# Two input tiles, then the first conditioning group, then the other tiles: a new order at the head of a one-layer decoder step

## What is computed

```python
mod = jnp.einsum('bd,de->be', jax.nn.silu(c), w_ada) + b_ada
sh1, sc1, g1, sh2, sc2, g2 = [m[:, None, :] for m in jnp.split(mod, 6, axis=-1)]
h = x * (1 + sc1) + sh1
z = jnp.einsum('btd,de->bte', h, w_in) + b_in
a_glu, q, k, v, qi, ki, wi, uv, gate_logits = jnp.split(z, SPLIT_OFFSETS, axis=-1)
```

## Time and profile before

| | |
|---|---|
| median of 3 runs | 1046.58 us (1044.06 to 1046.66) |
| the profiled execution's own time | 1057.31 us |
| its span, first to last instruction | 1055.4 us |
| TensorE busy | 998.1 us (95%) |
| VectorE busy | 548.5 us (52%) |
| ScalarE busy | 198.9 us (19%) |
| GpSimd busy | 254.2 us (24%) |
| mean granted clock of TensorE | 0.970 |
| moved by DMA | 214.98 MB, mean 204 GB/s |

### The profile page before, as it was taken

One profiled execution on the slowest core, in us unless ns is written; L12 is line 12 of the kernel. 1 busy time (PEld: TensorE's weight loads), 2 busy tenths in 40 slices (PEclk: granted clock), 3 DMA queues, 4 the chain that ended last, 5 costly groups with the idle time before them and its releaser, 6 DMA issues. The chain is left out here.

```text
span 1055.4 us, 23402 instructions
## 1 busy us (share of the span) xinstructions
PE 998.1 (95%) x9475; PEld 719.8 (68%) x9475; DVE 548.5 (52%) x1381; ACT 198.9 (19%) x474; POOL 254.2 (24%) x284
## 2 busy tenths in 40 slices
PE   5999999999999999899999999977999999999995
PEld 4677777557776767576777764554776777677763
DVE  1131899984457888976456815687233121011137
ACT  1110012213222323232111110111111111111104
POOL 0010002824121223123335620000211212422123
PEclk8998999999999999899999999976999999999998
DMA  9964742653605215014072336242799999899995
GB/s 307 308 139 114 240 161 82 217 206 122 238 21 164 77 31 195 20 46 126 11 191 69 120 98 271 70 189 101 306 423 416 357 410 396 347 383 396 389 277 113
DMA packets 94003, 214.98 MB, mean 204 GB/s; under 512 B 23572, under 2 KB 48407, under 8 KB 89797
## 3 DMA queue, kind: packets, MB, share of 16 engines
q1 hardware_dynamic: 78388, 186.20, 49.5%
q0 software_dynamic: 6672, 19.67, 6.2%
q10 hardware_dynamic: 8841, 7.64, 2.6%
HBM read 201.12 MB, written 16.92 MB: 207 GB/s over the span
## 5 line engine op out<-in xcount | busy, mean ns | idle before, releaser
L2120 PE MATMUL banks<-arena 128*128 128x288 f32 (+6 forms) x1774 | 427.6, 396 | 6.3 <-issue 2.5
L2120 PEld LDWEIGHTS banks<-arena 128*128 128x128 f32 (+1 forms) x1774 | 317.1, 191 | 108.9 <-issue 32.4
L2520 PE MATMUL banks<-arena 128*32 128x256 f32 x3136 | 186.7, 384 | 4.1 <-issue 2.9
L2520 PEld LDWEIGHTS banks<-arena 128*32 128x32 f32 x3136 | 131.7, 110 | 48.5 <-issue 8.1
L2048 DVE TENSOR_TENSOR arena<-arena,banks 128x128 f32<-128x128 f32 x49 | 14.1, 288 | 222.7 <-ACT arena L1353 222.5
L2542 PE MATMUL banks<-arena 128*32 128x256 f32 x1568 | 100.2, 379 | 1.5 <-issue 0.8
L1051 POOL DMA_INDIRECT expert_rows<-arena,ints x44 | 43.0, 977 | 196.9 <-ACT arena L1364 192.8
L993 POOL TENSOR_SCALAR arena<-arena 128x288 f32<-128x288 f32 x46 | 44.9, 975 | 168.2 <-ACT arena L1275 102.1
L1430 DVE SCALAR_TENSOR_TENSOR arena<-arena 128x512 f32<-128x512 f32 x120 | 82.0, 743 | 0.0
L2542 PEld LDWEIGHTS banks<-arena 128*32 128x32 f32 x1568 | 61.5, 109 | 21.7 <-issue 6.4
L2134 PE MATMUL banks<-arena 128*128 128x288 f32 x256 | 69.9, 431 | 2.7 <-DVEq L1448 2.7
(11 more groups left out here) (321 smaller groups left out, 998.4 us busy)
## 6 DMA issues: line engine op xcount, KB each, us to landing
arena<-in_w_e_gate SPq DMA_DIRECT2D x16, 2048.0 KB
arena<-in_w_e_up SPq DMA_DIRECT2D x16, 2048.0 KB
arena<-in_w_e_down SPq DMA_DIRECT2D x16, 2048.0 KB
arena<-in_w_ada SPq DMA_DIRECT2D x8, 2048.0 KB, 10.3
arena<-in_w_in SPq DMA_DIRECT2D x8, 2048.0 KB, 9.7
arena<-in_w_ada SPq DMA_DIRECT2D x8, 1024.0 KB, 11.6
arena<-in_x_prompt SPq DMA_DIRECT2D x8, 512.0 KB, 7.0
arena<-in_w_in SPq DMA_DIRECT2D x14, 256.0 KB, 8.2
```

Source lines behind the costliest of these rows:

```text
L2120: last = pe.matmul(out, a, b, start=k == 0, stop=k == len(pairs_) - 1)
L2520: last = pe.matmul(out, HG[:, g % 2, k, a:a + BLK], both_weights(i, k, c), start=k == 0, stop=k == KT - 1)
```

## The change

In the list of steps, conditioning group 0 moves ahead of tiles 2 and 3, the samples and the parameters, and ahead of all halves 1, which move behind `acc 0`. In SP's order, the two loads of group 0 move ahead of those of tiles 2 and 3, the samples and the page ids. Nothing is computed anew and no bytes are added.

```diff
-    plan = [("cT",)] + [("xT", t, z) for t in range(4) for z in range(2)] + [("xTs",), ("par",), ("adp", 0), ("mT", 0), ("mod", 0)]
+    plan = [("cT",), ("xT", 0, 0), ("xT", 1, 0), ("adp", 0), ("xT", 2, 0), ("xT", 3, 0), ("xTs",), ("par",), ("mT", 0), ("mod", 0)]
     for g in range(3):
-        plan += [("acc", 2 * g, 0, 6), ("adp", g + 1), ("acc", 2 * g + 1, 0, 3), ("mT", g + 1), ("mod", g + 1), ("acc", 2 * g + 1, 3, 6)]
+        plan += [("acc", 2 * g, 0, 6)] + ([("xT", t, 1) for t in range(4)] if g == 0 else []) + [("adp", g + 1), ("acc", 2 * g + 1, 0, 3), ("mT", g + 1), ("mod", g + 1), ("acc", 2 * g + 1, 3, 6)]
     plan += [("acc", 6, 0, 6)]
@@
         for t in range(NT):
+            if t == 2:
+                first_conditioning(0)
             src = I["x_prompt"][0, t * P:t * P + P, :] if t < 4 else I["x_sample"].rearrange("b t f -> (b t) f")
             sp.dma_start(X[0:rows_of(t), t, :], src).then_inc(ev(f"tile_in{t}"), 16)
@@
         for g in range(4):
-            first_conditioning(g)
+            if g > 0:
+                first_conditioning(g)
             a_columns(2 * g, 2, slice(0, P), f"a_in{g}")
             a_columns(2 * g, 2, slice(512, 512 + 2 * P), f"a_in{g}")
```

## The result

The changed kernel takes 1052.39 us (median of 20 runs), the kernel before 1049.21 us (20 runs beside them). The ratio is 1.0036 with a 95% interval of 1.0023 to 1.0049, that is +3.8 us (+2.4 to +5.1); the plain difference of the two medians is +3.2. The forecast was +3.8 us, which made 1050.4 on the three runs then known. The direction and the size of the difference held. Several terms of the sum did not, and that their errors nearly cancelled is luck.

The account below looks back on a forecast made before the run. TensorE was taken to bound the kernel, its head passing through nearly one to one: +0.3 us at `acc 0` and +3.8 for second-half flips made +4.1, reduced to +3.8 over the 1046.58 us median: 1050.4 us, range 1046.5 to 1053.

Parts of the forecast that it names:

- The bound: After 32 us TensorE bounds the kernel, so what its head gains or loses goes through nearly one to one.
- The landing of `adp 0`: First conditioning group's load, issued behind tile 1, lands at 17.5 us instead of 21.3, kept late by the conv weights' packets.
- Half clock at `adp 0`: After TensorE's wait the first conditioning group again runs at half clock, taking 3.64 us, to 21.1 us.
- Flips, samples and hand-over to VectorE's `mT`: Behind `adp 0`: 2.8 us of flips, samples and parameters at full clock, 1.55 us to VectorE's `mT`, +0.6 for the clock.
- From there to `acc 0`: From VectorE's `mT` to the start of the first projections: 1.71 us, as in the kernel before.
- `acc 0`: First projections start at 27.8 us, 0.3 later than before, and keep their length of 4.87 us, mostly at half clock.
- The second halves: Four groups of flips between `acc 0` and `adp 1`, 1.90 us for two: 3.8 us, all on the path.
- The second halves in under 3 us: Sign of a wrong prediction: the four groups of flips behind `acc 0` take less than 3 us.
- The sum at `adp 1`: Second conditioning group starts 4.1 us later, at about 36.4 instead of 32.35 us: +0.3 at `acc 0`, +3.8 for flips.
- The early landing: Rival, chance 0.11: `adp 0` lands early enough to win, at 13.8 us by bytes; 1043.5 to 1046.3 us.
- The clock's rival: Rival, chance 0.19: clock does not fall at `acc 0`, which takes 3.19 us; +1.8 us in all, 1048.3 us.
- the cold case: Rival, chance 0.13: flips behind `adp 0` wholly at half clock, second halves partly; +5.8 to +7.5 us, 1052.4 to 1054.1.

Follow-up runs that it names:

- e4: Changed kernel with the conv weights' load cut into 16 and 15 rows; 1.0014 of the time of the kernel before (+1.5 us).
- e5: Kernel before with the conv weights' load cut into 16 and 15 rows; 0.9982 of the time of the kernel before (-1.9 us).
- e7: Kernel before with idle matmuls in TensorE's waits ahead of the parameters, `adp 0` and `acc 0`; 0.9973 of the time before (-2.8 us).
- e10: Changed kernel with six idle matmuls ahead of `adp 0` and two ahead of `acc 0`; 1.0007 of the time before (+0.7 us).
- e3: Changed kernel with the second halves of tiles 0 and 1 flipped ahead of `adp 0`; 1.0012 of the time before (+1.3 us).
- e6: Changed loads, conv load cut; tiles 0 and 1's second halves and parameters ahead of `adp 0`, `mT` right behind it; 0.9968 of the time before (-3.4 us).

## Why the prediction was right, step by step

- *The bound* held: a shift of the head goes through, as the table's two columns of differences show for all ten kernels, each within its interval. The intervals are 2.7 to 5 us wide, so this holds no closer than that.
- *The landing of `adp 0`* was taken at 17.5 and was 18.8 us: 1.3 us mis-sized. The reason given for its lateness, the conv weights' packets, was the right one (e4), but their price was taken from the old order, where the cut is worth 1 to 2 us; in the new one it is 3.2 to 4.2.
- *Half clock at `adp 0`*: 3.64 us, as forecast. *Flips, samples and hand-over to VectorE's `mT`*: 22.62 to 26.78 = 4.2 us, forecast 2.8+1.55 and 0.6 for the clock, 0.8 us too much: the flips ran at full speed, and the 2.8 us were a pace of half clock already (see below). *From there to `acc 0`*: 1.71 us, as forecast. `acc 0` started at 28.49, forecast 27.8: +1.5 from the release of `adp 0` (18.98 us for 17.5), -0.8 from the flips and the hand-over.
- *`acc 0`* was left at 4.87 us and took 5.68. The step weighed only a change of the clock for the better. The half clock at this step lasts differently long from kernel to kernel (4.58 to 6.11 us for the twelve records where it does not stay away); what sets that is open.
- *The second halves* failed in size: 3.8 forecast, 2.8 measured. "The second halves in under 3 us" stood among the prediction's own signs of being wrong, and it came: they are exposed, as the forecast says, but cheaper. The 1.90 us for two were read from the stretch at 9 to 15 us, which I took to be at full clock because the column said so. But eight flips at 6.34 us took 1.97 us, and here, at 34.01 us, 1.03: the head of the kernel before was at half clock too, and what I took for the pace of full clock was not.
- The sum at `adp 1` was +4.1 and is +4.48: +0.7 from the start of `acc 0`, +0.7 from its length (from its start to the next step's 5.52 us, before 4.80), -1.0 from the second halves. The near agreement is luck.
- *The rivals.* The early landing (at 13.8 us) did not come, but e4 shows that it was to be had: with the conv weights' load cut it is 14.6 us, and the change is then level in the head with the kernel before as it was (not with that kernel and the same cut, e5). The clock's rival did not come in the profiled execution; it came in two of the eight kernels without idle matmuls, and was put at 0.19. e7 and e10 show what full clock at both steps is worth at `adp 1`: some 3.4 us in the old order (2.6 and the 0.7 of the later release) and 4.3 in the new (4.1-0.8+1.0, for the earlier release and for what the idle matmuls took). What the cold case named, flips at half clock, did not come (and it took the second halves at 3.4 us, where the forecast has 3.8); what grew was the half clock at `acc 0` itself, which no case had priced.
- The Trainium skill's rule on work cut up by waits (TensorE: Matmul & The Clock Gate, section "HAM oscillation — how this bites in real kernels") pointed to the cold case; e7 shows the rule at work, with 1.7 us at `adp 0` and 1.7 at `acc 0`, though the wait ahead of `acc 0` is one for VectorE and not for a load. Since both orders have both waits it speaks only a little against the change.

## What to carry to other kernels

A step that stands in a wait is free, and moving a critical load forward empties that wait of its cheap work: first count what is left to fill the new, longer wait, and put there whatever already has its inputs (e3, e6). When a load lands late for its bytes, look for a small transfer of another queue in the same time and try it cut: 31 rows as 16 and 15 brought `adp 0` 3.2 to 4.2 us forward in the new order of loads, more than that order did (2.5 us), and 1 to 2 us in the old. Where two orders both wait, compare them at the same clock before the order gets the credit or the blame.

## What the runs showed of the hardware

- The granted clock is printed as 1.00 at the head of the span also where the instructions run at half speed: 3.64 us for the 64 records of `adp 0` in the changed kernel at a printed 1.00, 1.96 us for the same records in e7. Durations of equal instructions are the better witness there.
- One load of 31 rows of 2 KB (62 KB) on ScalarE's queue went with a later landing of the 2 MB of `adp 0` on SP's queue: whole 18.1 to 18.8 us (four kernels), as 16 and 15 rows 14.6 and 14.9 (two), in the new order of loads; 21.0 to 22.1 (three) and 19.8 to 20.0 (two) in the old.
- With idle matmuls in the wait ahead, `adp 0` (1.96 us) and `acc 0` (3.19 us) ran at full speed, 2.4 GHz, in three kernels of three. They are not free everywhere: in e10 those ahead of `acc 0` ran at half speed and held it back by about 1.0 us.
- Single runs of the kernel before differ by up to 10 us. The places found in the traces are the length of the half-clock stretch at 90 us (1.4 us) and the expert stage (6.5 us), in part of which the DMA engines moved about a third of what they moved in the other kernel; the cause of that stays open.
